# A two-block transformer kernel in exact fp32 halves: the mixture of experts on tiles of gathered tokens, inside the stream, in place of all tokens in stages of their own

## What is computed

```
x = x + merged @ w_out
h2 = rms_norm(x, norm_ffn)
x = x + hierarchical_moe(h2, ...)
h3 = rms_norm(x, norm_ple)
x = x + sigmoid(h3 @ w_ple_gate) * (p @ w_ple)

def hierarchical_moe(t, ...):                       # t: (512, 1024)
    p_group = softmax(t @ w_rg + b_rg)              # (512, 4)
    g_idx = argmax(p_group)                         # one group per token
    w_in_group = the two largest of softmax(expert logits of that group), made to sum to 1
    combine = one_hot(g_idx) * p_group[g_idx] * w_in_group
    for gi in range(4):
        act = silu(t @ w_gate[gi]) * (t @ w_up[gi]) * combine[:, gi]
        y = y + act @ w_down[gi]                    # summed over the group's 4 experts
```

## Time and profile before

| | us |
|---|---|
| median of 3 runs (lowest, highest) | 3803.95 (3801.78, 3813.26) |
| the profiled execution | 3810.55 |
| its span in the trace | 3808.7 |
| PE busy, share of the span | 3477.9, 91% |
| DVE busy, ACT busy | 1757.5 (46%), 1181.9 (31%) |
| bytes moved by DMA | 256.61 MB |
| mean granted clock of PE | 0.947 of full |

### The profile page before, as it was taken

The page is one execution under the profiler, slowest core; times in us unless marked ns, Lnnn a source line. Parts: engine busy times, 40 slices in busy tenths (PEclk is TensorE's granted clock), DMA queues, the critical chain, the costliest instruction groups (busy, mean ns, idle before and its releaser), DMA issues. The chain is left out here.

```text
span 3808.7 us, 41353 instructions
## 1 busy us (share of the span) xinstructions
PE 3477.9 (91%) x16406; PEld 2736.0 (72%) x16406; DVE 1757.5 (46%) x2500; ACT 1181.9 (31%) x1804; POOL 0.2 (0%) x4
## 2 busy tenths in 40 slices
PE   7988999999999899999999998689799949989986
PEld 5556867888856687788887776468688838778774
DVE  3354535554344553555433445666445434424423
ACT  2233224332213322333223445343524222112212
POOL 0000000000000000000000000000000000000000
PEclk9989999999989899999999999889899969999998
DMA  4111013333311100233332121110002213323322
GB/s 143 39 34 55 24 46 98 94 100 93 118 48 33 54 28 28 86 97 97 111 102 83 56 66 41 33 33 29 28 28 78 78 45 88 88 80 94 87 61 69
DMA packets 163009, 256.61 MB, mean 67 GB/s; under 512 B 7968, under 2 KB 112032, under 8 KB 162464
## 3 DMA queue, kind: packets, MB, share of 16 engines
q1 hardware_dynamic: 161264, 247.05, 22.1%
q10 hardware_dynamic: 1584, 7.31, 0.5%
HBM read 252.24 MB, written 2.10 MB: 67 GB/s over the span
## 5 line engine op out<-in xcount | busy, mean ns | idle before, releaser
L627 PE MATMUL bank<-h_head,flow_head 128*128 128x512 f32 x2112 | 897.2, 425 | 27.2 <-DVE flow_rest L655 24.8
L655 DVE TENSOR_TENSOR flow_rest<-flow_raw,flow_head 128x1024 fp32r<-128x1024 f32 (+2 forms) x372 | 438.4, 1179 | 964.1 <-ACT flow_head L644 964.0
L628 PE MATMUL bank<-h_rest,flow_head 128*128 128x512 f32 x2112 | 838.6, 397 | 0.0
L629 PE MATMUL bank<-h_head,flow_rest 128*128 128x512 f32 x2112 | 838.5, 397 | 0.0
L644 ACT ACTIVATE flow_head<-flow_raw 128x1024 fp32r<-128x1024 f32 (+2 forms) x372 | 379.2, 1020 | 738.7 <-PE bank L629 738.6
L627 PEld LDWEIGHTS bank<-h_head,flow_head 128*128 128x128 f32 x2112 | 406.1, 192 | 153.0 <-issue 70.2
L629 PEld LDWEIGHTS bank<-h_head,flow_rest 128*128 128x128 f32 x2112 | 405.4, 192 | 89.0
L628 PEld LDWEIGHTS bank<-h_rest,flow_head 128*128 128x128 f32 x2112 | 406.4, 192 | 87.6 <-issue 16.0
L244 PE MATMUL bank<-h_head,w_head 128*128 128x512 f32 x576 | 231.2, 401 | 48.4 <-DVE w_rest L222 48.4
L245 PE MATMUL bank<-h_rest,w_head 128*128 128x512 f32 x576 | 230.0, 399 | 0.0
L246 PE MATMUL bank<-h_head,w_rest 128*128 128x512 f32 x576 | 229.6, 399 | 0.0
(11 more groups left out here) (525 smaller groups left out, 4920.8 us busy)
## 6 DMA issues: line engine op xcount, KB each, us to landing
flow_raw<-in_w_in SPq DMA_DIRECT2D x176, 512.0 KB, 3.6
flow_raw<-in_w_gate_up SPq DMA_DIRECT2D x88, 512.0 KB, 3.6
flow_raw<-in_w_down SPq DMA_DIRECT2D x32, 512.0 KB, 3.5
raw<-in_e_gate SPq DMA_DIRECT2D x32, 512.0 KB, 4.2
raw<-in_e_up SPq DMA_DIRECT2D x32, 512.0 KB, 5.4
raw<-in_e_down SPq DMA_DIRECT2D x32, 512.0 KB, 5.3
flow_raw<-in_w_out SPq DMA_DIRECT2D x24, 512.0 KB, 3.6
flow_raw<-in_paths SPq DMA_DIRECT2D x24, 256.0 KB, 2.6
```

Source lines behind the costliest of these rows:

```text
L627: nc.tensor.matmul(ps[u.bank][:, :], wh, head, start=t == 0, stop=False)
L628: nc.tensor.matmul(ps[u.bank][:, :], wh, rest, start=False, stop=False)
L629: last = nc.tensor.matmul(ps[u.bank][:, :], wr, head, start=False, stop=t == len(u.columns) - 1)
L655: nc.vector.tensor_tensor(self.w_rest[:, n % 2, 0:w], self.raw[:, n % RAW_SLOTS, 0:w], f32(self.w_head[:, n % 2, 0:w]), ALU.subtract).then ...
```

## The change

All stages behind the stream are gone and their work joins it. The semaphores are cleared at the very end.

- **Router inside `w_out`.** Behind each `w_out` chunk a token unit follows: 3 matmuls of logits, 4 transposes of `x·gain`, a copy, and a DMA (from ACT's queue) that writes the chunk to a table `h_rows` in DRAM, one row per token. The last two token units come behind the last `w_out` chunk. Then tokens are counted by group with small matmuls and DVE operations, and each gets a place in one of 7 tiles of 128 rows; a tile holds tokens of one group only. There are 7 tiles whatever the tokens choose. Tiles 4 to 6 take their group from registers.
- **Gathered tiles.** GpSimd gathers each tile (indirect DMA, 128 rows of 4 KB) into `picked`; PE transposes it (8 transposes), ACT and DVE split it.
- **Experts, 28 (tile, expert) pairs.** The tile stands in PE and the weights move. Up is 8 columns of 3 matmuls, gate and up side by side in one bank; a tanh and two DVE operations on 128x256; two transposes; head and rest; down is 4 columns of 3 matmuls. A group's 4 experts add up in two banks.
- **Weights** come in blocks of 1 MB (8 KB per partition, three per pair, 84 in all) into a ring of 9 buffers, of which each is split as two pieces; two more head and rest slots (`late_head`, `late_rest`) stand beside the stream's two.
- **Back.** A tile's result is copied out (`y_tile`) and stored by GpSimd into `y_rows`; after the last, four indirect DMAs fetch each token's row, 32 transposes bring them back, and DVE adds them to `x_t`.
- **Embedding.** 48 matmuls of the path product run while that goes on; the gate product takes `x·gain` without the root, which is applied at eviction; the result is stored in 8 pieces of 256 KB.

Cut to its core (lines of the changed kernel):

```
-    block_2_end(nc, ps, ring, dram, xT, (head, rest), views(pk_2, PARAMS_2), base)
...
+    k.ring = [at(f"ring_{n}", c, (2048,)) for n, c in enumerate((52, 56, 60, 64, 48, 28, 32, 36, 40))]
...
+def expert_up(k, i, dram):
...
+    j, e, q = i // EXPERTS, i % EXPERTS, i % 2
+    pieces = load_expert(k, i, 0, dram) + load_expert(k, i, 1, dram)
...
+        nc.scalar.activation(k.glu_th[q][:, :], k.ps[bank][:, 0:256], ACT.Tanh, scale=w[:, 0:1]).then_inc(*k.late["glu_squashed"].up())
...
+    def gate(v, m):
+        v.wait_ge(*k.late["glu_squashed"].at(i + 1))
+        k.dve_chain(nc.vector.scalar_tensor_tensor(k.glu_th[q][:, :], k.glu_th[q][:, :], 1.0, k.ps[bank][:, 0:256], ALU.add, ALU.mult))
+        nc.vector.scalar_tensor_tensor(k.glu[q][:, :], k.glu_th[q][:, :], w[:, 1 + e:2 + e], k.ps[bank][:, 256:512], ALU.mult,
+                                       ALU.mult).then_inc(*k.late["glu_done"].up())
...
+def expert_turn(k, i):
+        for f in range(2):
+            last = nc.tensor.transpose(k.ps[6][:, f * P:(f + 1) * P], k.glu[q][:, f * P:(f + 1) * P], k.const["ident"])
...
+                if u.rows:
+                    nc.tensor.matmul(ps[bank][:, :], head, wh[:, c:c + S], start=start, stop=False)
+                    nc.tensor.matmul(ps[bank][:, :], head, wr[:, c:c + S], start=False, stop=False)
+                    last = nc.tensor.matmul(ps[bank][:, :], rest, wh[:, c:c + S], start=False, stop=stop)
...
+    n = TILES * EXPERTS
...
+    for i in range(n):
+        if i + 2 < n:
+            expert_up(k, i + 2, dram)
+        if i + 1 < n:
+            expert_turn(k, i + 1)
+        expert_down(k, i, dram)
...
+    def pick(j):
+        if j >= 2:
+            g.wait_ge(flow.products, flow.units[k.tile_unit[j - 2]].done)
+        nc.gpsimd.indirect_dma_start(
+            out=k.picked[j % 2][:, :], out_offset=None, in_=h_rows,
+            in_offset=bass.IndirectOffsetOnAxis(ap=k.indices[:, j:j + 1], axis=0)).then_inc(*k.picked_landed[j % 2].up(16))
...
+    for j in range(TILES):
+        if j + 2 < TILES:
+            pick(j + 2)
+        g.wait_ge(*k.late["y_kept"].at(2 * j + 2))
+        nc.gpsimd.dma_start(y_rows[j * P:(j + 1) * P, :], k.y_tile[j % 2][:, :]).then_inc(*k.y_stored[j % 2].up(16))
+    for m in k.y_stored:
+        g.wait_ge(m.sem, m.total)
+    for t in range(NT):
+        nc.gpsimd.indirect_dma_start(
+            out=k.back[t][:, :], out_offset=None, in_=y_rows,
+            in_offset=bass.IndirectOffsetOnAxis(ap=k.positions[:, t:t + 1], axis=0)).then_inc(k.back_landed[t][0], 16)
```

More of the change, by code:

```diff
@@ new lines, in slot_weights_unit, with turn, keep @@
+def slot_weights_unit(k):
+    nc, flow = k.nc, k.flow
+    def turn(pe, m):
+        pe.wait_ge(*k.late["moe_scaled"].at(1))
+        for t in range(NT):
+            last = nc.tensor.matmul(k.ps[0][:, 0:TILES * 5], k.places[:, t, :], k.scales_is[:, t, :], start=t == 0, stop=t == NT - 1)
+        return last
+    def keep(v, m):
+        v.wait_ge(flow.products, flow.units[m].done)
+        nc.vector.tensor_copy(k.slot_w[:, :], k.ps[0][:, 0:TILES * 5]).then_inc(*k.late["moe_slots"].up())
+    flow.unit(None, [], None, [(-.4, keep)], turns=turn, free=[], ticks=1)
@@ new lines, in tile_units, with turn, four, heads @@
+def tile_units(k, j, half):
+    nc, flow, n = k.nc, k.flow, 2 * j + half
+    bank = 6 if n == 1 else 7
+    c0, c1 = 4 * half, 4 * half + 4
+    def turn(pe, m):
+        if half == 0:
+            pe.wait_ge(*k.picked_landed[j % 2].at(16 * (j // 2 + 1)))
+        if n >= 2:
+            pe.wait_ge(*k.late["tile_rests"].at(n))
+        for c in range(c0, c1):
+            last = nc.tensor.transpose(k.ps[bank][:, (c - c0) * P:(c - c0 + 1) * P], k.picked[j % 2][:, c * P:(c + 1) * P],
+                                       k.const["ident"])
+        return last
+    def four(t):
+        return t[j % 2][:, c0:c1, :]
+    turned = k.ps[bank][:, :].rearrange("p (c n) -> p c n", n=P)
+    def heads(a, m):
+        a.wait_ge(flow.products, flow.units[m].done)
+        nc.scalar.activation(four(k.tile_head), turned, ACT.Copy).then_inc(*k.late["tile_heads"].up())
+    def rests(v, m):
+        v.wait_ge(*k.late["tile_heads"].at(n + 1))
+        nc.vector.tensor_tensor(four(k.tile_rest), turned, f32(four(k.tile_head)), ALU.subtract).then_inc(*k.late["tile_rests"].up())
+    k.tile_unit[j] = flow.unit(None, [], None, [(.5, rests)], [(.4, heads)], turns=turn, free=[], ticks=1)
@@ new lines, in load_expert, with first, src @@
+def load_expert(k, i, b, dram):
+    flow = k.flow
+    j, e, n = i // EXPERTS, i % EXPERTS, len(k.ring_pieces)
+    def first(sp):
+        if n < RING:
+            sp.wait_ge(*k.ring_free[n]())
+        if j >= 4 and not k.group:
+            sp.wait_ge(*k.late["moe_groups"].at(1))
+            k.group += [sp.value_load(k.groups[0:1, q:q + 1], min_val=0, max_val=3) for q in range(3)]
+    def src(sp):
+        if j < 4:
+            return dram["experts"][j, e, b]
+        return dram["experts"][bass.ds(k.group[j - 4], 1), e, b, :, :].rearrange("o p n -> p (o n)")
+    used = k.ring_pieces[n - RING] if n >= RING else []
+    k.ring_pieces.append(flow.block(k.ring[n % RING], src, k.late_landed[n % RING], used, first, [k.late_slot() for _ in range(2)]))
+    return k.ring_pieces[-1]
@@ L3086, in block_2_end @@
[L3086 to L3094 removed]
+    flow.loads()
```

1008 lines of the change are left out of this document (545 added, 463 removed).

## The result

The changed kernel takes 3428.52 us (median of 4 runs, 3425.49 to 3430.53), against 3805.11 for the kernel before on the same chip: a ratio of 0.9007, 95% interval 0.899 to 0.9023. Forecast were 3416, within 3385 to 3480.

What follows compares the result with a forecast made beforehand. PE was taken to bound the kernel, busy for 91% of the span. Terms 3052.6 + 6.7 + 24.7 + 254.5 + 82.5 gave a span of 3421.0 us, 387.7 less, so a median of 3416, range 3385 to 3480.

Steps and rivals of the forecast that it cites:

- The work: Experts: 8192 token-experts become 3584, so 2304 matmuls of 128x512 before become 1008 after, each 0.225 us at full clock.
- `w_out`, +6.7: Last stage of the stream: six token units inside it add 6 x 1.12 us, so its last product comes at 3059.3.
- The handover, 24.7: From the last `w_out` product to the first expert product: a chain of router and first gather, 24.7 us against 76.5.
- The pairs, 9.0 each: 28 (tile, expert) pairs: PE's 8.55 us plus 5% gives 9.0 each, 252 us; 254.5 with a restart, against 570.3.
- the 5% on it: Expert pairs: matmuls at 0.236 us, as in the old expert stage, not 0.225, raising PE's 8.55 us to 9.0.
- The restart at half clock: Start of the expert pairs: 15 matmuls take 5.84 us where full clock gives 3.4, so 2.5 us more.
- The tail, 82.5: From the last expert product to the end: stores, gathers back, norm, gate product and semaphore clears, 82.5 us against 109.3.
- The engines wait for one another: Expert pairs: one ring piece's rest per pair stands in PE's way, 10.1 us a pair, 32 more, 3448; chance 0.20.
- Transfers bound it: Expert pairs: at 300 GB/s, 91.3 MB of transfers take 304 us, 50 more, 3466; chance 0.10.
- Half clock in every pair: Expert pairs: each pair has a wait that costs 2.5 us of restart, 70 more, 3486; chance 0.05.
- GpSimd's DMAs are slow: First gather and last store take 10.7 us, not 3.6, and four fetches back run in a row: 22 more, 3438; chance 0.09.
- One at a time: Weight ring: a block's transfer begins only when the last is split, 9.0 us a block, 502 more, 3918; chance 0.01.

## Why the prediction was right

The span was forecast at 3421.0 and came out at 3428.7; the median at 3416 and 3428.5. The second distance is larger because the kernel before has a median 4.75 us under its profiled span, and the changed one's stands 0.2 under it. That the distance is no larger is in part luck: the handover was 13.1 us too short in the sum and the pairs 8.3 too long.

**The work.** Right: 1296 matmuls less, at the price of the old stage, are 322 of the 324 us.

**`w_out`, +6.7.** Measured +6.9. What was not in it: ACT's wait for a token store, 2.4 us, of which PE felt 0.8.

**The handover, 24.7.** This is the term that failed: 37.8. The step "ACT's copy of token unit 6, its DMA issue ...; the same for unit 7" priced the copy and the issue, and not the wait for a buffer whose store was still under way. The run with buffers of their own puts 9.8 of the 13.1 us on it, and the run with the blocks held shows why the store was late. The prediction had the gather's landing as its unknown between 0 and 10.7; the gather stayed well inside (5.5 us from indices to transposes, and 5.3 with a plain DMA), and the danger was in the DMA before it, about which it had not asked. The other 3.2 us, in the run with own buffers: the logits begin 1.2 later than summed, the step to the indices takes 0.4 more, from the indices to the transposes it is 5.7 and not 3.6, and the first product follows 0.6 sooner.

**The pairs, 9.0 each.** Measured 8.7 ((246.2 - 2.5) / 28). PE's 8.55 was nearly right and the 5% on it, taken from the old expert stage, was not: PE had no gap in 220 us. Why the old stage's gaps are absent (ring, slots, or the length of its loop) was not tested. DVE's 8.4 proved right when PE was relieved (8.35), ACT's 7.1 a little high (6.9). DMA's 7.9 was near (7.6), from 91.3 MB where the DMA view has 88.3 in the stretch. The restart at half clock is there: 13 slow matmuls from 3098.55 on. It costs more than 2.5 us: the prediction counted 15 matmuls in 5.84 us where there were 14 from start to start, and here 14 took 6.08, 2.9 more than at full clock.

**The tail, 82.5.** Measured 84.0, by parts that were off both ways. Up to the last transposes' row it took 14.4 us where 12.2 stood: the copies and the store 5.0 for 5.2, the four fetches 9.4 for 7.0. The norm took 2.5 less than priced (17.4 us to the last product that a rest releases, for 19.9). PE's part behind it took 2.9 more (41.6 for 38.7), and 2.1 of these are the granted clock, which the sum had left out: in the two runs in which it was back at 1.00 sooner, this part took 39.5 and 39.6. The end behind the last gate product took 10.6 for 11.7.

**The rivals.** *The engines wait for one another*: no, 8.7 and not 10.1. *Transfers bound it*: no; at 300 GB/s they would have, but the big blocks move at 384, and at 418 when PE and DVE are relieved. The 411 of the first 16 us of the trace was the better guide than the rate over share of the old stream. The Trainium skill ("DMA: Bandwidth & Descriptors", Specifications) puts a core's HBM share at about 358 GB/s; the trace shows more over 180 us, on a chip with one core at work. *Half clock in every pair*: no, clock 1.00; but it came back once in the tail. *GpSimd's DMAs are slow*: no, and its work did not slow DVE's rests either (1.22 us each, and 8.35 a pair where 8.4 was summed from the old rows), so the contention between the two that the Trainium skill names ("GPSIMD Engine Reference", Key points) doesn't show here, where all that GpSimd does is to issue DMAs, 7.3 us of 220. *One at a time*: real, priced at 9.0 and measured at 8.4 a block, but only with one buffer.

## What to carry to other kernels

When a step is moved beside other work, price not only its instructions but also the buffer that its DMA gives back: a small store that lands in 2 us alone took 12 beside megabyte loads, and the engine behind it stood still. A resource that reads 98% busy need not bind; the way to know is to take work from one at a time. A gain of the expected size need not come from the expected cause: in the tail PE's granted clock moved 2 us about, and only the windows around the edit told it from DVE's work. And when work is left out, the price of what remains is first looked for in the old stage's own rows, before any gain from the new order is counted.

## What the runs showed of the hardware

- One core's DMA moved 384 GB/s over 220 us and 418 over 180, in blocks of 8 KB per partition. Its small stores (256 KB, 128 words at a time) landed in 2.3 to 14.5 us in the changed kernel, and with one ring buffer in 2.3 to 7.0.
- An indirect DMA of 128 rows of 4 KB costs GpSimd some 1 us to issue, against 0.5 for a plain one. At the handover the transposes that need the first of them begin 4.4 us after its issue, and 4.5 with plain ones.
- DVE's two gate operations, both on 128x256 with one input from PSUM, took 0.41 us with a constant (L2947) and 0.48 with a scalar per partition (L2948).
- PE's granted clock in the 7 us around the last rest of the norm was 0.55, 0.86 and 1.00 in three kernels whose queues for PE are the same there. The last two had the last gate product 2.1 us sooner behind the norm.
